# Two blocks of a hybrid transformer in float32 on one core: the attention's products of probabilities and values issued as two half-width products each

## The reference, cut to what matters

```
s = jnp.einsum('bgrqd,bgkd->bgrqk', q, k) * scale
p = masked_softmax(s, valid)
o = jnp.einsum('bgrqk,bgkd->bgrqd', p, v)
```

## Time and profile before

| | |
|---|---|
| median of three runs | 2104.4 us |
| the profiled execution | 2107.1 us |
| its span, first to last instruction | 2105.3 us |
| PE busy | 2035.1 us, 97% |
| PEld busy | 1891.8 us, 90% |
| DVE busy | 1340.7 us, 64% |
| ACT busy | 1001.7 us, 48% |
| granted TensorE clock, mean | 0.997 |

### The profile page before, as it was taken

How to read it: one execution, slowest core, us unless ns; L and a number is a source line. 1 busy time by engine, 2 the same in 40 slices (tenths; PEclk the granted TensorE clock), 3 DMA queues, 4 the chain that set the end, 5 groups by cost and what they waited for, 6 DMA issues and landing times. The chain is left out here.

```text
span 2105.3 us, 41276 instructions
## 1 busy us (share of the span) xinstructions
PE 2035.1 (97%) x17378; PEld 1891.8 (90%) x17378; DVE 1340.7 (64%) x1985; ACT 1001.7 (48%) x1433; POOL 13.0 (1%) x12
## 2 busy tenths in 40 slices
PE   7999999999999999999999989999999999999998
PEld 7999987999999998799989979989998888998997
DVE  6555565754655466575547666578777857577775
ACT  5333456533534345553436544455455544456543
POOL 0000000000000000000000010000000010000000
PEclk9999999999999999999999999999999999999999
DMA  7543722554454372265344324366544333347551
GB/s 300 200 179 111 247 108 84 220 201 163 185 230 189 127 231 81 72 237 207 154 165 163 128 87 141 111 218 237 207 159 151 127 110 112 122 151 280 192 188 51
DMA packets 79875, 348.89 MB, mean 166 GB/s; under 512 B 21232, under 2 KB 30576, under 8 KB 45808
## 3 DMA queue, kind: packets, MB, share of 16 engines
q1 hardware_dynamic: 79728, 346.74, 44.9%
HBM read 345.67 MB, written 1.05 MB: 165 GB/s over the span
## 5 line engine op out<-in xcount | busy, mean ns | idle before, releaser
L89 PE MATMUL bank<-ffn_hT_split,n_split_gate_up 128*128 128x256 f32 x1408 | 391.7, 278 | 2.8 <-DVE ffn_hT_split L199 2.4
L90 PE MATMUL bank<-ffn_hT_split,n_split_gate_up 128*128 128x256 f32 x1408 | 391.1, 278 | 0.0
L91 PE MATMUL bank<-ffn_hT_split,n_split_gate_up 128*128 128x256 f32 x1408 | 391.0, 278 | 0.0
L89 PEld LDWEIGHTS bank<-ffn_hT_split,n_split_gate_up 128*128 128x128 f32 x1408 | 265.9, 189 | 5.2 <-issue 3.7
L90 PEld LDWEIGHTS bank<-ffn_hT_split,n_split_gate_up 128*128 128x128 f32 x1408 | 266.1, 189 | 1.5
L91 PEld LDWEIGHTS bank<-ffn_hT_split,n_split_gate_up 128*128 128x128 f32 x1408 | 265.6, 189 | 0.0
L363 ACT ACTIVATE work<-bank 128x256 f32<-128x256 f32 x88 | 33.2, 383 | 311.6 <-PE bank L91 311.5
L1808 DVE TENSOR_TENSOR mix_parts<-mix_arrived,mix_parts 128x1024 fp32r<-128x1024 f32 x88 | 107.6, 1224 | 93.4 <-ACT mix_parts L1803 93.3
L462 DVE TENSOR_TENSOR work<-bank,work 128x256 f32<-128x256 f32 x88 | 37.3, 423 | 190.4 <-ACT work L363 190.4
L443 DVE TENSOR_TENSOR ffn_split_down<-ffn_arrived_down,ffn_split_down 128x2048 fp32r<-128x2048 f32 x44 | 100.9, 2292 | 80.7 <-ACT ffn_split_down L358 80.7
L426 DVE TENSOR_TENSOR n_split_gate_up<-arrived_gate_up,n_split_gate_up 128x2048 fp32r<-128x2048 f32 x64 | 144.5, 2287 | 9.5 <-ACT n_split_gate_up L348 9.5
(11 more groups left out here) (386 smaller groups left out, 5761.8 us busy)
## 6 DMA issues: line engine op xcount, KB each, us to landing
arrived_gate_up<-in_ffn SPq DMA_DIRECT2D x64, 1024.0 KB, 8.4
ffn_arrived_down<-in_ffn SPq DMA_DIRECT2D x44, 1024.0 KB, 4.8
mix_arrived<-in_mix_w SPq DMA_DIRECT2D x88, 512.0 KB, 3.5
rrived_gate_up<-in_conv_ffn SPq DMA_DIRECT2D x32, 1024.0 KB, 6.8
_arrived_gate_up<-in_ffn SPq DMA_DIRECT2D x24, 1024.0 KB, 6.7
mixer_arrived<-in_w_in SPq DMA_DIRECT2D x22, 1024.0 KB, 7.2
onv_ffn_arrived_down<-in_conv_ffn SPq DMA_DIRECT2D x22, 1024.0 KB, 4.8
irst_project_arrived<-in_w_in SPq DMA_DIRECT2D x17, 1024.0 KB, 4.8
```

The source lines that it names most:

```text
L89: pe.matmul(out, lhs[0], rhs[0], start=start, stop=False)
L90: pe.matmul(out, lhs[0], rhs[1], start=False, stop=False)
L91: return pe.matmul(out, lhs[1], rhs[0], start=False, stop=stop)
```

## The change

Each product of `add` is issued through `matmul_halves`, at the place in the order where it stood. Nothing else is changed: the same weights, the same values, the same accumulation over the key tiles, and the semaphore is raised by the last instruction as before.

```diff
             for kt in range(t + 1):
-                last = pe.matmul(sum_bank(t, b)[:, h * DH:(h + 1) * DH], probsT[u % 3][:, kt * P:(kt + 1) * P],
-                                 c.vtok[:, kt, v:v + DH], start=(kt == 0), stop=(kt == t))
+                last = matmul_halves(pe, sum_bank(t, b)[:, h * DH:(h + 1) * DH], probsT[u % 3][:, kt * P:(kt + 1) * P],
+                                     c.vtok[:, kt, v:v + DH], start=(kt == 0), stop=(kt == t))
             last.then_inc(s["added"], 1)
```

## The result

The changed kernel is slower, by more than was forecast. The first comparison had five executions of each: median 2124.3 us (2116.5 to 2127.0) against 2104.4, ratio 1.0081 with a 95% interval of 1.0063 to 1.0100. The forecast was 2115.5 in a range of 2109 to 2121. Over all four, 23 executions of it, the difference of the means is +16.7 us with a standard error of 1.0, weighted by the precision of each. Single executions scatter by about 4 us (a standard deviation of 3.9 for the kernel before, 2.4 to 6.3 for the variants); 95 of the kernel before average 2106.9, so the 2104.4 that the forecast started from was 2.5 us low.

The account below looks back on a forecast made before the run. TensorE was taken to bound the kernel, busy 97% of the span. Unit terms summed to 5.54 us a layer, +11.1 us for two, so the median 2104.4 would become 2115.5 us, range 2109 to 2121.

Parts of the forecast that it names:

- The price of a unit: Each `add` call in attention: +0.095 us in front, +0.06 (one product) or -0.055 (two) within, +0.085 or -0.055 behind.
- The kinds and their counts: Of 48 units a layer, 9 at +0.10, 13 at +0.24, 7 at -0.015, 13 at +0.125 us: 5.54 us.
- The passages that no row showed: From halves to 512 column form, rotation's product or transposes: +0.085 us each assumed, bounds 0 and +0.15.
- The cover: Six units a layer in front of TensorE's waits priced at nothing; if that failed, 1 us a layer more.
- No DMA is moved: Claim that the change moves no transfer anywhere in the kernel; nothing was counted for it.
- The clock, "2 us either way": Second block: where TensorE's clock falls to 1.2 GHz can shift by chance; 2 us allowed either way.
- The start: The median time of the kernel before, 2104.4 us, to which the forecast added its 11.1 us.
- Free passages: Rival for attention's products: halves pay at their run's pace, 0.116 us, passages hide; -15 us, 2089; chance 0.05.
- Serial halves: Rival for attention's products: halves run one after the other, 0.116 us more each; +15 us on top, 2130; chance 0.05.
- More cover: Rival: DVE and ACT set the attention's pace, so TensorE's additions shorten its idle time; 2108 us; chance 0.06.

Follow-up runs that it names:

- each tile alone: Kernel before with halves only in tile 1's units (two products): +4.8 +- 1.4 us; only in tile 0's units (one product): +5.9 +- 1.2 us.
- the three other comparisons: The changed kernel measured again with no edit, each time beside the kernel before: ratios 1.0071, 1.0083 and 1.0097.

## Why the prediction was right in its mechanism and wrong in its time

*The price of a unit.* Right, in each of its three parts. The mixers of the changed kernel are 10.7, 11.1, 11.0 and 10.9 us longer in four traces, where the sum gave 11.1. The passages were priced from places where halves stood in long runs, and held for single units.

*The kinds and their counts.* Right: each tile alone came within 0.3 us of its own sum. The passages that no row showed, into the 512 column projection and others, cost +0.09 from the last half on, as they were priced.

*The cover.* Right as far as can be seen: PE's waits for L932 stayed at 2.7 us, and the sum fits with the units ahead of them at nothing (1 us a layer otherwise).

*"No DMA is moved."* This is the step that failed: the term was put at nothing. No transfer of the kernel's own was moved, but TensorE's instructions are transfers too, and 576 more of them put one packet of the instruction queue against `sg_w_s` at a barrier, where PE soon has nothing else to do. The transfer lands 1.3 to 2.0 us later, and in two of the four traces of the change more of the work behind it runs at the lower clock: the second mix is 2.8 to 6.8 us longer in the four traces of the change, 4.5 in the mean. With 10.9 from the mixers that is 15.4, against 16.7 +- 1.0 measured. That adding instructions brings the delay about and adding some more takes it away is shown; why one packet holds the transfer up is not.

This sum takes two stages and not the whole. The four traced executions of the change have spans of 2114.0 to 2118.1 us, only 8.7 to 12.8 over the one trace of the kernel before: its other stages together are 4.7 to 6.8 us shorter than in that one trace, which is among the longest there. And each of the four lies below the mean of its own run, by 2.4 to 10.8 us. So the untraced executions take longer than the traced ones; that they lose it in the same stretch is argued from their lower grant, and not shown.

*The clock, "2 us either way".* Too small, and taken for chance alone. One trace differs from the next by more than that in a single stage (second mix of the change: 313.4 to 317.4 us), and the mean grant is lower in the kernels whose transfer is late (0.9936 against 0.9954 in the kernel before).

*The start.* 2104.4 was the median of three executions that scatter by 4 us; the kernel before averages 2106.9 over 95. 2106.9 + 10.9 + 4.5 is 2122.3; the changed kernel's 23 executions average 2123.4. Of the 7.9 us between that and the forecast, 2.5 are the start. In the first comparison itself the kernel before stood at 2104.4 too, so the start explains nothing of the 19.9 us between its two medians; the three other comparisons alone give 16.1 +- 1.2 by their means.

*The rivals.* Free passages: no, they cost what they cost elsewhere. Serial halves: no, the starts of the two halves are 7 ns apart, in pairs. (Its count of 126 products is 124 by the prediction's own counts, which leaves its 2130 as it is.) More cover: no, the waits stayed.

## What to carry to other kernels

Price a change of tiling by the passage, not by the product: here the passages in and out cost 0.18 us, a first product in halves 0.06 more, and each further one gave 0.10 back, so halves pay in runs of several and not one unit at a time. A change that adds instructions to an engine also moves its instruction packets: look at what stands behind each barrier, where a small transfer is waited for with nothing to cover it, and compare variants that differ by a few dozen instructions before a few microseconds are put down to the change itself. A median of three says little where single executions scatter by 4 us.

## What the runs showed of the hardware that was not expected

- One 16 KB packet of the instruction queue among some 600 others delayed a 256 KB transfer from 2.9 to between 4.2 and 4.9 us, six times in six.
- With a delay of 1.3 to 2.0 us at that place the stage was 2.8 to 9.5 us longer. How much more than the delay goes with the clock: in the trace with 9.5 us the mean grant of the 20 us from the start was 0.57, in the one with 2.8 it was 0.92.
- PE's busy time in the attention's products fell by 5.0 us while the stage grew by 11: the two halves of a product start 7 ns apart and overlap, and passages between tilings are not counted as idle.
